# One-core transformer pair on Trainium2: sixteen experts of 128 slots against twelve groups of four 32-column tiles with 96 slots an expert, and layer norms in two fused passes

## What is computed

```python
for l in range(2):
    mix = even_mixer(...) if l % 2 == 0 else odd_mixer(...)
    x = layer_norm(ALPHA * x + mix, ln_g[l, 0], ln_b[l, 0])
    # routed_moe: each token takes the best 2 experts of the best group of 4, of 16 experts
    for e in range(16):
        h = silu(xt @ w_gate[e]) * (xt @ w_up[e])     # 1024 -> 512
        y = y + gates[:, e:e + 1] * (h @ w_down[e])   # 512 -> 1024
    x = layer_norm(ALPHA * x + y, ln_g[l, 1], ln_b[l, 1])
```

## Time and profile before

| | us |
|---|---|
| median of 3 runs (lowest, highest) | 2345.96 (2340.42, 2351.76) |
| the profiled execution | 2345.56 |
| its span | 2343.9 |
| mean granted TensorE clock, of full speed | 0.934 |

### The profile page before, as it was taken

The page is one execution under the profiler, slowest core; times in us unless marked ns, Lnnn a source line. Parts: engine busy times, 40 slices in busy tenths (PEclk is TensorE's granted clock), DMA queues, the critical chain, the costliest instruction groups (busy, mean ns, idle before and its releaser), DMA issues.

```text
span 2343.9 us, 17929 instructions
## 1 busy us (share of the span) xinstructions
PE 2117.7 (90%) x6662; PEld 1035.4 (44%) x6662; DVE 680.3 (29%) x1566; ACT 423.5 (18%) x897; POOL 114.2 (5%) x119
## 2 busy tenths in 40 slices
PE   7999999999999999799799999919988979999990
PEld 3464444444444444354544444415444454444440
DVE  4734422222003300442500000053865260000005
ACT  3221011111000210452111111111154211111111
POOL 0000100000000000000010000030000001000003
PEclk9989999999999999869799999958998979999995
DMA  3116322222121130004388898730000527898843
GB/s 141 54 37 228 122 72 73 88 81 73 54 72 66 50 129 0 1 1 162 113 305 319 334 333 320 272 135 2 35 1 1 198 99 282 321 341 322 322 175 135
DMA packets 143012, 343.84 MB, mean 147 GB/s; under 512 B 4776, under 2 KB 12984, under 8 KB 142816
## 3 DMA queue, kind: packets, MB, share of 16 engines
q1 hardware_dynamic: 126384, 283.80, 33.8%
q0 software_dynamic: 11664, 40.38, 4.5%
q10 hardware_dynamic: 4896, 18.75, 2.0%
HBM read 316.13 MB, written 26.76 MB: 146 GB/s over the span
## 4 chain that ended last, share of the span: by engine, by line
PE 87%; DVE 5%; ACT 2%; issue 2%; DMA 2%; POOL 0%; POOLq 0%; DVEq 0%; another core or an unknown queue 0%; ACTq 0%; PEldq 0%; SPq 0%
PE psum L519 63%; PE psum L762 7%; PE psum L699 4%; PE psum L828 3%; PE psum L856 2%; PE psum L841 2%; PE psum L898 1%; DVE x L1494 1%; DVE small L1523 1%; PE psum L641 1%; PE psum L531 1%; ACT ring L1325 1%; PE psum L931 1%; DMA scratch<-expert_rows,place 0%; DMA expert_rows<-scratch 0%
## 5 line engine op out<-in xcount | busy, mean ns | idle before, releaser
L519 PE MATMUL psum<-ring,scratch 128*128 128x512 f32 x1696 | 749.2, 598 | 10.7 <-issue 4.3
L519 PEld LDWEIGHTS psum<-ring,scratch 128*128 128x128 f32 x1696 | 318.7, 191 | 395.3 <-issue 391.0
L519 PE MATMUL psum<-xT,ring 128*128 128x512 f32 (+2 forms) x1056 | 463.7, 600 | 8.3 <-PE psum L519 3.4
L519 PEld LDWEIGHTS psum<-xT,ring 128*128 128x128 f32 (+2 forms) x1056 | 199.0, 190 | 270.4 <-issue 269.5
L519 PE MATMUL psum<-ring,xT 128*128 128x512 f32 (+4 forms) x704 | 239.6, 497 | 2.5 <-ACTq L1092 1.6
L519 PEld LDWEIGHTS psum<-ring,xT 128*128 128x128 f32 x704 | 120.3, 194 | 119.8 <-issue 111.6
L762 PE MATMUL psum<-ring,scratch 128*128 128x512 f32 x352 | 154.4, 599 | 4.0 <-remote 3.3
L2014 DVE TENSOR_TENSOR scratch<-psum,scratch 128x512 f32<-128x512 f32 x32 | 22.1, 692 | 435.2 <-PE psum L519 435.2
L1494 DVE SCALAR_TENSOR_TENSOR scratch<-psum,overlay,scratch 128x511 f32<-128x511 f32 x88 | 65.9, 749 | 230.5 <-ACT scratch L1256 228.9
L762 PEld LDWEIGHTS psum<-ring,scratch 128*128 128x128 f32 x352 | 66.9, 192 | 90.8 <-issue 90.8
L699 PE MATMUL psum<-xT,ring 128*128 128x512 f32 x224 | 101.7, 609 | 2.4 <-DVEq L1483 2.3
(11 more groups left out here) (330 smaller groups left out, 1549.2 us busy)
## 6 DMA issues: line engine op xcount, KB each, us to landing
ring<-in_moe_w_gate SPq DMA_DIRECT2D x32, 2048.0 KB, 8.6
ring<-in_moe_w_up SPq DMA_DIRECT2D x32, 2048.0 KB, 11.4
ring<-in_moe_w_down SPq DMA_DIRECT2D x32, 2048.0 KB, 10.1
ring<-in_w_up SPq DMA_DIRECT2D x11, 2048.0 KB, 10.5
expert_rows<-scratch ACTq DMA_DIRECT2D x32, 512.0 KB, 7.4
ring<-in_w_down SPq DMA_DIRECT2D x4, 2048.0 KB, 7.7
ring<-in_even_w_in SPq DMA_DIRECT2D x4, 2048.0 KB, 7.8
ring<-in_w_o SPq DMA_DIRECT2D x4, 2048.0 KB, 9.6
```

The source lines that it names most:

```text
L519: mm = nc.tensor.matmul(out_, lhsT, rhs, start=(j == 0), stop=(j == len(pairs) - 1))
```

## The change

Each expert has 96 slots (`CAP`), three tiles of 32 columns. The 48 tiles of 16 experts are packed in `NG` = 12 groups of four; group g holds tiles of the experts `(4 * g + i) // 3`. A group is one pass of the old kind, but each of its products is issued as four of 32 columns: the same slab of the group's turned rows, 32 tokens of it, as stationary operand at its own 32 columns of the array, and the tile's own expert's weights (128x512) as moving operand. Loops become straight code. The weights' tiles go to seven buffers, the six of the ring and `xT`; a buffer is reloaded once the last group that uses it has. The routing finds group and slot of a token by comparing its place with multiples of 128. The layer norm becomes two passes, `(x - mu) * G` and `r * that + B`, both on DVE. The next 128 tokens of an expert over 96 would go to an overflow slot, of which there are up to 10.

```diff
+TILE = 32
+CAP = 3 * TILE
+NG = E * CAP // P
...
+            def tiled(bank, lhsT, nk, views, c0=0):
+                for t in range(nk):
+                    for i, w_ in enumerate(views):
+                        r = slice(i * TILE, (i + 1) * TILE)
+                        mm = nc.tensor.matmul(bank[r, :], lhsT[:, t, r], w_[:, t, c0:c0 + 512],
+                                              start=(t == 0), stop=(t == nk - 1))
+                return mm
...
             def experts(l):
+                turn_x(l, 0)
+                for g in range(NG):
+                    enter(l, g)
+                    if g:
+                        leave(l, g - 1)
+                    turn_h(l, g)
+                leave(l, NG - 1)
...
+        PASSES = [p for g in range(NG) for p in [("gate", g), ("up", g)] + ([("down", g - 1)] if g else [])] + [("down", NG - 1)]
+        FIRST_FREE = [(5, 2, 0, 1, 3, 4, RING), (2, 3, 0, 1, 4, 5, RING)]
...
+                for m, e, b, freed in loads_of[l]:
+                    if freed:
+                        m_, g = freed
+                        if m_ == "down":
+                            sp.wait_ge(y_done, 2 * (NG * l + g) + 2)
+                        else:
+                            sp.wait_ge(gate_up_done, 2 * (NG * l + g) + (1 if m_ == "gate" else 2))
+                    elif b == RING:
+                        sp.wait_ge(routed, NT * (l + 1))
...
+                if not root_mean:
+                    centred = begun(V.scalar_tensor_tensor(x[:, n, :], x[:, n, :], mu, rowsG, ALU.subtract, ALU.mult))
                 dve.wait_ge(tile_sd, base + 1)
                 step(V.reciprocal(r, r))
...
-                    step(V.tensor_scalar(x[:, n, :], x[:, n, :], mu, r, ALU.subtract, ALU.mult))
-                    gained = V.tensor_tensor(x[:, n, :], x[:, n, :], rowsG, ALU.mult)
...
+                    V.scalar_tensor_tensor(x[:, n, :], x[:, n, :], r, rowsB, ALU.mult, ALU.add).then_inc(tile_ready, 1)
...
+                V.scalar_tensor_tensor(token_here, rank_of, float(CAP), operand["token_f"].unsqueeze(1).to_broadcast([P, 2, NT]),
+                                       ALU.is_lt, ALU.mult)
+                step(V.tensor_tensor(flat(place_f), flat(rank_of), flat(first_place), ALU.add))
+                step(V.tensor_tensor(past, both(place_f, NG - 1), ..., ALU.is_ge))
+                step(V.tensor_reduce(flat(group_of_place), past, AX.X, ALU.add))
+                step(V.tensor_tensor(hot_group, both(group_of_place, NG), ..., ALU.is_equal))
+                V.tensor_tensor(group_token, hot_group, both(token_here, NG), ALU.mult)
+                step(V.scalar_tensor_tensor(flat(place_f), flat(group_of_place), -float(P), flat(place_f), ALU.mult, ALU.add))
```

More of the change, by code:

```diff
@@ L918, in leave, with weights_of @@
[L918 to L929, removed]
+            def weights_of(l, m, g):
+                views = []
+                for e in experts_of(g):
+                    b, loads = buffer_of[l][m, e]
+                    pe.wait_ge(expert_loaded[b], loads)
+                    views.append(expert_buffer(b, 4 if m == "down" else KD))
+                return views
@@ new lines, in tiled, with enter @@
+            def tiled(bank, lhsT, nk, views, c0=0):
[5 more added lines that the diff above has]
+                return mm
+            def enter(l, g):
+                pe.wait_ge(xgT_ready, 2 * (NG * l + g) + 2)
+                for j, m in enumerate(("gate", "up")):
+                    tiled(banks[2 + j], xgT, KD, weights_of(l, m, g)).then_inc(gate_up_done, 1)
+                if g < NG - 1:
+                    turn_x(l, g + 1)
@@ L930, in turn_h, with leave @@
+            def leave(l, g):
+                at = NG * l + g
+                pe.wait_ge(hT_ready, at + 1)
+                views = weights_of(l, "down", g)
+                for j in range(2):
+                    if at:
+                        pe.wait_ge(y_taken, 2 * at - 1 + j)
+                    tiled(banks[5 + j], hidT, 4, views, j * 512).then_inc(y_done, 1)
+            def turn_h(l, g):
+                pe.wait_ge(h_ready, NG * l + g + 1)
                 for t in range(4):
@@ L1340, in attend, with take_x @@
                         take_out((i - 6) // 4)
-            def take_x(done):
-                for g in range(2):
-                    act.wait_ge(xgT_done, done + g + 1)
-                    A(xgT[:, 4 * g:4 * g + 4, :].rearrange("p a b -> p (a b)"), banks[g][:, :], ACT.Copy).then_inc(xgT_ready, 1)
+            def take_x(at):
+                for h in range(2):
+                    act.wait_ge(xgT_done, 2 * at + h + 1)
+                    A(xgT[:, 4 * h:4 * h + 4, :].rearrange("p a b -> p (a b)"), banks[h][:, :], ACT.Copy).then_inc(xgT_ready, 1)
@@ new lines, in experts @@
+                for g in range(NG):
+                    at = NG * l + g
+                    act.wait_ge(gate_up_done, 2 * at + 1)
+                    A(silu_g, banks[2][:, :], ACT.Silu).then_inc(silu_ready, 1)
+                    if g < NG - 1:
+                        take_x(at + 1)
+                    if g:
+                        leave(l, g - 1)
+                leave(l, NG - 1)
+                for b in range(2):
+                    act.wait_ge(y_stored[b], 16 * (NG // 2) * (l + 1))
@@ L2310, in load @@
                     sp.wait_ge(w_used, at - RING + 1)
+                    if 0 <= at - first_expert_chunk[0] < RING:
+                        m, g = max((holder for holder in last_held if holder[0] == at % RING), key=lambda h: h[1])[2]
+                        sp.wait_ge(y_done if m == "down" else gate_up_done, 2 * g + (1 if m == "gate" else 2))
                 dst = ring[:, at % RING, 0:src.shape[1] * src.shape[2]].rearrange("p (k n) -> p k n", k=src.shape[1])
```

239 lines of the change are left out of this document (96 added, 143 removed).

## The result

The change takes 2188.45 us (median of 4 runs, 2185.77 to 2197.15), the kernel before, timed beside it, 2348.86 (4 runs, 2340.42 to 2353.12): ratio 0.933, interval 0.929 to 0.937, so about 160 us less. A second set of runs beside the first experiments gave 2183.12 (2181.37 to 2190.06). The forecast of 2180 us is 8 us from the first median and 3 from the second, inside the range. The profiled execution took 2186.29 us, its span is 2184.6.

What follows compares the result with a forecast made beforehand. The expert stage was taken as bound by PE, with DMA close behind. From 2345.56 us, expert stages -155.4, layer norms -13.8 and routing +4.0 gave 2180 us, with a range of 2150 to 2280.

Steps and rivals of the forecast that it cites:

- Four tiles at once: Expert stage on PE: four 32-column products take the time of one, 0.43 us a set, as attention's pairs do.
- B: Expert stage: the four tiles' weight loads take turns, a set 0.52 us, a round 27.6, total 2276 us; chance 0.06.
- C: Expert stage: four streams don't fit, two do; a set 0.86 us, a round 43.7, total 2662 us; chance 0.06.
- D: Expert stage: tiled products keep PE at half clock, a round about 45 us, total 2693 us; chance 0.05.
- E: Overflow: an expert over 96 tokens is done alone, some 50 us; chance 0.03 together with anything not seen.
- Two ways in and out of the tile mode a round: Expert stage on PE: switching between tiled products and whole-array transposes costs 0.5 us a round, giving a period of 23.1.
- DMA at 385 GB/s: Expert stage: the 98.6 MB left to move take 256 us at this pace; stage end at 276 us by DMA alone.
- rival A: Expert stage: DMA queue gives only 333 GB/s as before, 315 us a layer, total 2241 us; chance 0.12.
- Waits for weights: Expert stage: PE waits 1 to 4 us at groups 6 and 9 for late tiles; 285 us a layer taken.
- the walk: Expert stage: load order followed, each tile issued when its buffer's pass ends; 286 us at 380 GB/s, 281 at 390.
- Norms: Layer norms in combine: 7.3 us a tile instead of 8.90, 6.9 us a layer, 13.8 us less together.
- Routing: Seven DVE instructions ahead of the token list and two small top-2 ones: 2.0 us a layer, 4 us more.

Runs made afterwards that it cites:

- The last pair of runs: Eight-buffer kernel with the odd layer's static tiles waiting for layer 0's combine gathers, 2165.29 us, beside the eight-buffer kernel once more, 2175.35 us.

## Why the prediction was right

Right in the mechanism and within 8 us in size, but its terms missed by more than the sum did.

- **Four tiles at once.** Taken from pairs, it holds for four: sets 0.43 us apart, granted clock 0.99 over 200 us of the first stage. Rivals B (sets of 0.52 us), C (0.86) and D (clock of 0.5) are excluded by the timeline and the windows, and E by the timeline, which has no products between the end of the stage and combine. The page "TensorE: Matmul & The Clock Gate", Part 3, of the Trainium skill has 3.07 times the pace for four row tiles and 2.38 for three column tiles. Here four column tiles in a stream have 4.0 times (four records every 0.43 us), and the measurement decides.
- **Two ways in and out of the tile mode a round**: 0.5 us taken, 0.57 measured, shown by whole-array products. PE's chain: 278.5 taken, 277.1 measured. The round came out at 22.5 where 23.1 stood, since the base of 22.55 was the longer of two values that alternate before, 22.1 and 22.5; whole-array rounds in straight code take 21.9. Filling and emptying took 7 us (277.1 less 12 rounds of 22.5) where 1.3 stood (2.3 less the 1.0), so two misses of 6 to 7 us, in the rounds and at the ends, nearly cancelled inside this term; that it came within 1.4 us is luck.
- **DMA at 385 GB/s**: 396 over 200 us of the stage, so rival A falls. The step from windows of 10 us to such a stretch held. The Trainium skill, "DMA: Bandwidth & Descriptors", "Where 436 GB/s comes from", has some 358 GB/s bind a load from memory, a figure that it gets by halving the rate of a memory stack that two cores share; this trace has 396 GB/s for a core alone and disagrees with it there.
- **Waits for weights**: the term that was mis-sized. 6.5 us a stage were taken (285 - 278.5), and the stages have 10.4 and 12.9 us above PE's chain. The waits alone are 8.6 and 8.7 us, at groups 3, 6 and 9 where the walk had 6 and 9, and that with a faster queue than it assumed. The other 2 and 4 us are a term that the prediction has nowhere: behind a wait PE runs at a lower clock (0.84 over the pass of 8.39 us). Six buffers show the same weakness: the walk gave 5 to 6 us for a buffer less, and it was 19, with waits of 23 us for 14. It sees which pass frees a buffer, but not how far a late tile pushes all that follow in the queue; that this is the reason is argued, not shown. Stages: 577.5 us where 570 stood.
- **Norms**: 6.93 us a tile where 7.3 stood; the last combine and output 8.2 us shorter where 6.9 stood, and alone in the kernel before 12 us in all, for 13.8. The wait for ACT's root is covered wholly.
- **Routing**: the seven operations between the list's reduction and its use add 1.5 us a layer (1.83 against 0.32 us from start to start), and two small ones 0.17 each nearby; 1.6 to 1.9 for 2.0.
- **The missed term**: SP's order. The prediction has nothing for the time between the end of a stage and combine; SP's order cost 4.6 us there after the first layer, through a static tile that waits for the last down pass's buffer with five others behind it. The last pair of runs shows that these tiles slow the gathers.
- **What evened it out.** Against the terms, the spans have +7.9 us in the stages (0.4 of it from how the ends of before are read), +4.4 in the two gaps behind them, -2.6 in the norms and -0.8 in the routing. What is left, +2.8 us ahead of the first stage and about -5.8 us in the second layer's attention, is drift in work that the change doesn't touch. The first part came and went with the same code (1164.8 and 1159.8 us); with the second goes the granted clock, 0.89 from the first pass of combine to the second stage in this trace, 0.87 before (see the last section). The sum is 5.9 us, the difference between 165.2 us forecast and 159.3 measured; half a dozen terms of either sign stand behind it, so its smallness is partly luck.

## What to carry to other kernels

Where each set of weights is used by few rows, column tiles that are issued in turn give four independent streams for the time of one, at the cost of a change of mode now and then; issued one chain after another they give little (rounds of 60.6 us in place of 22.5). Once PE no longer bounds a stage, count the buffers: with transfers of 5 us and passes of 7, one buffer was worth 19 us a stage at six and some 5 at seven; and a wait can cost more than it lasts, since the clock was lower behind it. And whoever shortens a stage should look at what the queues release at its end: the loads for the next stage, freed all at once, stood in the way of a short store and of gathers that everything waited for.

## What was not expected of the hardware

- **Partial overlap.** Tile by tile a round took 60.6 us, 24 us less than one after another. A round has 16 chains of products, so each change of tile hides three to four products of 0.43 us. So PE doesn't start them in the order of the program there: in the rows above, a product of the next tile starts at 1259.13, ahead of those of the tile before it that start at 1259.55 and later.
- **Reading at 396 GB/s without a fall**, for the 200 us of the window, while PE is busy for 191 of them: the DMA share stands at 1.04.
- **Attention wanders by 10 us.** With the same code, from the first pass of combine to the second expert stage it took 370.1 us (static tiles after the gathers) and 380.5 us (eight buffers once more). The windows over these stretches have nearly the same number of PE records and a granted clock of 0.89 and 0.85:

```profile
1460.42:1830.51 370.09, 310.90 (x1330) 171.59 (x1331) 219.12 (x608) 108.00 (x297) 7.22 (x11) 0.89 0.26 93
```

```profile
1466.09:1846.54 380.45, 322.16 (x1331) 179.47 (x1331) 219.54 (x609) 108.12 (x297) 6.30 (x10) 0.85 0.18 65
```

PE works there in many short pieces with pauses, and how long it then runs at half clock (1.2 GHz) differs from execution to execution: 0.85 rather than 0.89 over these stretches is, as an estimate, 25 to 30 us more at half clock. The runs with half weights and with the whole array took 381 us there too, at 0.85, and the first profile of the change 370.5 at 0.89. Why the clock falls for longer in some executions is open. A few us of this kernel can't be read from its total; they are read stretch by stretch.
